# Latent attention in one core's trunk: rotary keys and latent norms placed ahead of the second late modulation piece, the gate's sums placed behind two heads

## The chip, the cores and the metric

The kernel runs on 1 core of one Trainium2 chip. A time is the device time of one execution in microseconds (us). Three executions of the kernel before gave 882.97, 884.5 and 885.7 us; their median, 884.5 us, is what a change is measured against. The core has five engines, each with its own queue of instructions: TensorE (PE in the profile; PEld is its weight load), VectorE (DVE), ScalarE (ACT), GpSimd (POOL) and the sync engine (SP), which here only issues transfers. Engines wait for each other by semaphores.

## What is computed

A trunk of two layers on 256 tokens of width 1024, in float32. Layer 0 is retention and a mixture of experts; layer 1 is latent attention and a mixture of experts. Cut to the part around the change:

```python
mod = c_act @ w_mod[layer] + b_mod[layer]          # six vectors of 1024 for each layer
sh1, sc1, g1, sh2, sc2, g2 = jnp.split(mod, 6, axis=-1)
# layer 1
hn = modulate(rms_norm(h, norm_kv), sh_kv, sc_kv)
a = hn @ w_kv_a                                    # 128 latent + 64 rotary
c_kv = rms_norm(a[..., :128], kv_norm)
k_rope = rope(a[..., 128:])
k_nope, v = split(c_kv @ w_kv_b)                   # 8 heads of 128 + 128
q = rms_norm(modulate(rms_norm(h, norm_mix), sh1, sc1) @ w_q_a, q_norm) @ w_q_b
h = h + g1 * (attention(q, k_nope, k_rope, v) @ w_o)   # g1: the gate of this text
h = h + g2 * grouped_moe(modulate(rms_norm(h, norm_ffn), sh2, sc2), ...)
```

## The kernel before, in words

Every engine's order is written out by hand; nothing is planned at build time. Weights pass through a ring of six slots of 2 MB (`ring`) and some buffers beside it. SP issues the loads in one fixed order, each behind a wait for the use that frees its slot (`released`, L433), so one load that waits holds up all behind it. For layer 1 the order is `MLA_ITEMS` (L126): kva, qa, pieces 20 and 21, kvb, qb, pieces 22 to 25, wo0, wo1, pieces 26 and 27, then the experts' matrices of layer 1 (L483 to L504). Piece 25 takes the slot of piece 21 (freed when `mod_sum` reaches 22), wo0 that of kvb, wo1 that of qb, piece 26 that of piece 22 (`mod_sum` 23), piece 27 that of piece 23 (`mod_sum` 24).

A modulation vector of 1024 is one product of the activated c with a 1024 x 1024 block of `w_mod`. It comes in two pieces (an even and an odd number) of 2 MB. `mod_main` (L1527) has DVE multiply a piece in four quarters, each one instruction on 128x1024 elements that adds to a running sum in `part`; a step waits for the one before. The first quarter of an even piece writes without adding. Pieces 20 and 21 are vector 10, g1 of layer 1; 22 and 23 are vector 11 and 24 and 25 vector 12, shift and scale of the feed-forward of layer 1; 26 and 27 are its gate. What is left is a sum over the 128 partitions, which PE does: `gate_sum` (L610) for a gate (two matmuls of 128x512, one for each half, each two records in the profile), after which DVE's `gate_store` (L1553) adds the bias and stores it into `gate`; `row_sum` (L617) for a shift or scale. After the row sums of vectors 11 and 12 ACT copies the rows and sends them through two small transfers (`copy_rows(3)`, L1222, L1233, `turned<-y`), 4 KB each; DVE's `vectors(3)` (L1674, L1565) and ACT's L1302 wait for them.

The stage around the change, in the order of each engine:

- PE: `hnT` times kva (L1001, key latents and raw rotary keys), `xnT` times qa (L1009, query latents), with the transposes of the raw rotary keys between its halves (L1016); the two sums of vector 10 (L1021 to L1024), which wait for piece 21 and for the rotary products; transposes of the normed latents (L1027, L1032); key up-projection (L1041), its second half behind the gate's stores; value up-projection (L1048); query projections, rotary (L1058) and plain (L1070); then eight heads (L1115: scores L1082 and L1084, transposes of the probabilities L1095, values L1104 to L1106); then the output projection in blocks (L1130), with `row_sum(11)` behind the first block, `row_sum(12)` behind the fourth, and small matmuls of the router (L648, L800); then `experts(1)`, which turns h in four parts (L816), the last one behind `h_ready`.
- DVE: pieces 20 and 21, the rotary key products (L1842), the statistics of the latents (L1846, L1847), the normed latents (L1851, L1853), the query latents with their gain (L1856), the gate's stores (L1559), and then copies of keys and values with quarters of piece 22 between them, rotary query products (L1874), half of piece 23, in the heads the maxima and the scaling (L1881 to L1908), then the second half of piece 23 and pieces 24 to 27, the router's preparation (L1912, L1913), and in `mixed(1)` the four gated blocks of h (L1669), `vectors(3)` ahead of the last.
- ACT: `gate_bias(1)` (L1170, two transfers of the gates' biases into `gate`), modulation, copies of the raw rotary keys (L1360), squares of the latents (L1362, L1365), the root (L1367), the key latents with their gain (L1369), copies, exponentials.
- POOL: copies of the rotary columns of qb (L2071), the rotary keys (L2076 to L2081) behind the key products and the turned latents, the rotary queries (L2084).

Of the kernel before, what the change touches and what calls it, by code (L numbers as in the profile page):

```python
# [85 lines left out]
LATE_MOD = 20  # L86
# [4 lines left out]
MOD_STORED = {}  # L91
# [57 lines left out]
def build_kernel(nc, t, out):  # L149
    with ExitStack() as ctx:  # L150
# [139 lines left out]
        mla_bank = bank[4:] + bank[:4]  # L290
# [257 lines left out]
        def _(pe):  # L548
# [61 lines left out]
            def gate_sum(v, n, b=None):  # L610

                if b is None and (v > FIRST_MOD // 2 or n):
                    pe.wait_ge(mod_stored, MOD_STORED[(v, n)] - 1)
                b = bank[5] if b is None else b
                pe.matmul(b[:], ones, part[:, v % 2, n * 512:(n + 1) * 512], start=True, stop=True).then_inc(mod_folded, 1)
# [404 lines left out]

            pe.wait_ge(mod_sum, LATE_MOD + 2)  # L1021
            pe.wait_ge(kr_mult, 2)
            gate_sum(10, 0, mla_bank[5])
            gate_sum(10, 1, mla_bank[3])  # L1024
            pe.wait_ge(lat_norm, 2)
# [11 lines left out]
            for b in range(4):  # L1037
                if b == 2:
                    pe.wait_ge(mod_stored, MOD_STORED[(10, 1)])
                for j in range(2):  # L1040
                    ins = pe.matmul(mla_bank[1 + b][:, j * SEQ:(j + 1) * SEQ], kvb[:, 2 * b + j, 0:NOPE], ckT, start=True, stop=True)  # L1041
                ins.then_inc(kv_done, 1)
# [72 lines left out]
            for hd in range(MH):  # L1115
                if hd + 2 < MH:
                    scores(hd + 2)
                turn_probs(hd)
                if hd:
                    attend(hd - 1)  # L1120
            attend(MH - 1)

# [28 lines left out]
        def _(act):  # L1151
# [128 lines left out]
            def experts(l):  # L1280
# [71 lines left out]
              scale=rstd[:, 1:2]).then_inc(y1_ready, 1)  # L1352
            act.wait_ge(gb_in, 32)
            gate_bias(1)
            modulate(2, hnT, 4, MOD_COL[2])
# [12 lines left out]
            act.wait_ge(lat_turned, 1)  # L1368
            A(ckT, mla_bank[7][:, 0:SEQ], ACT.Copy, scale=lat_gain[:, 0:1]).then_inc(ckT_ready, 1)  # L1369
            act.wait_ge(rope_w, 1)  # L1370
            for b in (1, 3):
# [47 lines left out]
        def _(dve):  # L1419
# [416 lines left out]
            mod_main(20)  # L1836
            mod_main(21)

            dve.wait_ge(kr_raw, 1)
            for i in range(2):  # L1840
                w = trig[:, 1, i:i + 1, :].to_broadcast([P, 2, SEQ])
                dve.tensor_tensor(mprod[:, i, :].rearrange("p (f s) -> p f s", f=2),  # L1842
                                  mla_bank[5][:].rearrange("p (f s) -> p f s", f=2), w, ALU.mult).then_inc(kr_mult, 1)

            dve.wait_ge(lat_sq, 4)
            dve.tensor_scalar(var[:, 0:2], msq[:, 0:2], 1.0 / KVL, EPS, ALU.mult, ALU.add).then_inc(lat_ms, 1)  # L1846
# [8 lines left out]
            for j in range(2):  # L1855
                dve.tensor_scalar(qaT[:, j, :], mla_bank[0][:, j * SEQ:(j + 1) * SEQ], lat_gain[:, 1 + j:2 + j], None, ALU.mult).then_inc(qaT_ready, 1)  # L1856
            gate_store(10, 0, mla_bank[5])
            gate_store(10, 1, mla_bank[3])
            for b in (2, 4):
                mod_main(22, (b // 2 - 1,))  # L1860
                dve.wait_ge(rope_w, 1)
                dve.wait_ge(kv_done, b)
                dve.tensor_copy(knT[:, 2 * (b - 1):2 * b, :], mla_bank[b][:].rearrange("p (k s) -> p k s", k=2)).then_inc(kv_dve, 1)
            for b in (1, 3):
                dve.wait_ge(kv_done, 4 + b + 1)
                dve.tensor_copy(vm[:, b // 2, 512:1024], mla_bank[(5, 6, 7, 0)[b]][:]).then_inc(kv_dve, 1)
            mod_main(22, (2, 3))

            dve.wait_ge(kr_ready, 5)
            for f in range(2):  # L1870
                dve.wait_ge(qb_done, 1 + f)
                for i in range(2):
                    w = trig[:, 1, i:i + 1, :].to_broadcast([P, 2, SEQ])
                    dve.tensor_tensor(mprod[:, 2 * f + i, :].rearrange("p (f s) -> p f s", f=2),  # L1874
                                      mla_bank[5 + f][:].rearrange("p (f s) -> p f s", f=2), w, ALU.mult).then_inc(qr_mult, 1)
            mod_main(23, (0, 1))
            for b in (2, 4):
# [27 lines left out]
            for hd in range(MH):  # L1905
                head_scale(hd)
                if hd + 2 < MH:
                    head_max(hd + 2)  # L1908
            mod_main(23, (2, 3))
            for m in range(24, N_MOD):  # L1910
# [198 lines left out]
```

## Time and profile before

| | us |
|---|---|
| median of 3 runs | 884.5 |
| lowest, highest | 882.97, 885.7 |
| span of the profiled execution | 882.1 |
| PE busy | 839.5 (95%) |
| DVE busy | 329.5 (37%) |
| ACT busy | 177.4 (20%) |
| POOL busy | 159.5 (18%) |
| mean rate of the DMA engines | 360 GB/s |

The span is that from the first to the last instruction of one profiled execution; no separate time of that execution is given, so the span is what durations are summed against, and it lies 2.4 us under the median and 0.9 under the lowest run. Times in the views are microseconds from the start of the span. The stage of the change runs from about 512 to 592, the heads from 565.6 to 591, the output projection from 591.6 to 624, and the experts of layer 1 from 636.

### The profile page before, as it was taken

The numbers are of one execution on the slowest core, as the hardware profiler recorded it, in microseconds if no ns is written. First come the engines' busy times: TensorE is split into PE (matmuls) and PEld (weight loads), VectorE is DVE, ScalarE is ACT, GpSimd is POOL, SyncE is SP. The second block draws the span as 40 slices with busy tenths as digits, with TensorE's granted clock in tenths as the row PEclk, the third lists the DMA queues.
The fourth block names the chain that finished last, engine by engine and source line by source line (L and its number), as shares of the span: only waits on it lengthen the run. The fifth ranks groups of instructions, "written<-read, shape, count | busy, mean of one in ns | idle before, by whom it ended". The sixth has DMA issues, their size and how long they took to land.

```text
span 882.1 us, 11781 instructions
## 1 busy us (share of the span) xinstructions
PE 839.5 (95%) x4339; PEld 464.0 (53%) x4339; DVE 329.5 (37%) x598; ACT 177.4 (20%) x356; POOL 159.5 (18%) x269
## 2 busy tenths in 40 slices
PE   6999999999999999999999877999899999999996
PEld 4788444444444555455545445774545555545552
DVE  2825766955302322111112058778511112211114
ACT  2100113111102221122121141240322122112112
POOL 0023000000003521122210113300632211012111
PEclk9999999999999999999999998999999999999999
DMA  8989999998567699999999989929899999989994
GB/s 320 387 312 374 374 365 336 366 380 346 210 263 322 265 391 422 421 421 421 422 422 420 346 325 411 374 100 424 324 361 421 421 421 421 379 325 422 421 400 131
DMA packets 70014, 317.29 MB, mean 360 GB/s; under 512 B 10039, under 2 KB 10170, under 8 KB 44366
## 3 DMA queue, kind: packets, MB, share of 16 engines
q1 hardware_dynamic: 61594, 304.42, 86.1%
q0 software_dynamic: 4976, 8.40, 3.2%
q10 hardware_dynamic: 3396, 3.80, 1.3%
q8 instruction: 34, 0.56, 0.3%
q14 instruction: 14, 0.11, 0.0%
HBM read 311.31 MB, written 15.20 MB: 370 GB/s over the span
## 4 chain that ended last, share of the span: by engine, by line
PE 78%; DMA 9%; SPq 6%; DVE 3%; issue 1%; ACT 1%; ACTq 0%; POOL 0%; DVEq 0%; POOLq 0%
PE bank L735 12%; PE bank L914 10%; PE bank L901 10%; PE bank L932 10%; PE bank L776 6%; PE bank L876 6%; SPq L472 6%; PE bank L676 5%; DMA ring<-in_moe_w_down 3%; PE bank L1130 3%; DMA part<-outs 3%; DMA ring<-in_w_mod 2%; PE bank L728 2%; PE bank L557 1%; PE bank L1084 1%
## 5 line engine op out<-in xcount | busy, mean ns | idle before, releaser
L1793 DVE TENSOR_TENSOR arena<-bank,arena 128x256 f32<-128x256 f32 x34 | 20.9, 616 | 253.8 <-PE bank L914 253.8
L1543 DVE SCALAR_TENSOR_TENSOR part<-ring,cpad,part 128x1024 f32<-128x1024 f32 x84 | 111.1, 1323 | 3.3 <-DVE part L1543 0.5
L735 PE MATMUL bank<-ring,xnT 128*128 128x512 f32 x256 | 111.2, 592 | 0.0
L901 PE MATMUL bank<-ring,arena 128*64 128x512 f32 x416 | 92.1, 595 | 0.0
L914 PE MATMUL bank<-ring,arena 128*64 128x256 f32 x704 | 80.3, 381 | 0.2 <-issue 0.2
L932 PE MATMUL bank<-ring,arena 128*64 128x512 f32 x352 | 79.8, 595 | 0.0
L735 PEld LDWEIGHTS bank<-ring,xnT 128*128 128x128 f32 x256 | 48.4, 190 | 59.4 <-issue 59.3
L876 PEld LDWEIGHTS bank<-arena,y 128*128 128x128 f32 x544 | 63.7, 195 | 14.3 <-issue 14.3
L876 PE MATMUL bank<-arena,y 128*128 128x128 f32 x544 | 66.4, 281 | 0.0
L914 PEld LDWEIGHTS bank<-ring,arena 128*64 128x64 f32 x704 | 50.2, 137 | 30.1 <-issue 8.6
L1318 ACT ACTIVATE arena<-bank,modc,scale 128x128 f32<-128x128 f32 x68 | 25.6, 457 | 180.4 <-PE bank L876 176.4
L901 PEld LDWEIGHTS bank<-ring,arena 128*64 128x64 f32 x416 | 28.7, 137 | 52.2 <-issue 52.0
L1970 POOL DMA_INDIRECT outs<-arena,row_id x17 | 18.0, 1060 | 204.4 <-DVE arena L1813 123.7
L1946 POOL TENSOR_TENSOR h<-h,acc 128x512 f32<-128x512 f32 x6 | 7.6, 1267 | 242.0 <-DVE acc L1669 242.0
L1813 DVE SCALAR_TENSOR_TENSOR arena<-bank,info,gate 128x512 f32<-128x512 f32 x34 | 25.4, 751 | 66.3 <-PE bank L932 66.2
L1965 POOL TENSOR_SCALAR arena<-slot_id,place_two 128x64 f32<-128x64 f32 x108 | 45.9, 446 | 5.5 <-POOL slot_id L1980 3.0
L932 PEld LDWEIGHTS bank<-ring,arena 128*64 128x64 f32 x352 | 24.3, 137 | 41.1 <-issue 39.5
L676 PE MATMUL bank<-xnT,ring 128*128 128x256 f32 x192 | 41.9, 379 | 0.0
L676 PEld LDWEIGHTS bank<-xnT,ring 128*128 128x128 f32 x192 | 36.4, 190 | 5.3 <-DVE xnT L1496 0.5
L932 PE MATMUL bank<-arena 128*64 128x512 f32 x120 | 36.3, 596 | 0.0
L914 PE MATMUL bank<-arena 128*64 128x256 f32 x192 | 30.9, 397 | 4.0 <-DMA acc<-in_moe_w_up 4.0
L1784 DVE TENSOR_SCALAR arena<-bank,scale,modc 128x128 f32<-128x128 f32 x68 | 23.2, 406 | 23.6 <-PE bank L876 23.6
(342 smaller groups left out, 1067.6 us busy)
## 6 DMA issues: line engine op xcount, KB each, us to landing
ring<-in_w_mod SPq DMA_DIRECT2D x48, 1024.0 KB, 12.4
ring<-in_moe_w_gate SPq DMA_DIRECT2D x48, 1024.0 KB, 15.4
ring<-in_moe_w_down SPq DMA_DIRECT2D x44, 1024.0 KB, 13.2
ring<-in_moe_w_up SPq DMA_DIRECT2D x40, 1024.0 KB, 12.7
ring<-in_ret_w_in SPq DMA_DIRECT2D x24, 1024.0 KB, 7.5
arena<-in_moe_w_down SPq DMA_DIRECT2D x12, 1024.0 KB, 18.4
arena<-in_moe_w_up SPq DMA_DIRECT2D x12, 1024.0 KB, 17.7
arena<-in_moe_w_gate SPq DMA_DIRECT2D x9, 1024.0 KB, 10.0
```

The source lines that it names most:

```text
L472: sp.dma_start(home(l, m, f), w).then_inc(landed[f][b] if b < RING else outside_in[f][b - RING], 16)
L676: ins = pe.matmul(o[:, f * SEQ:(f + 1) * SEQ], w[:, k, c:c + P], xnT[:, k, :], start=(f == 0 and k == 0), stop=(f == 1 and k == KT - 1))
L735: ins = pe.matmul(pair[tt][:], xnT[:, k, tok(tt)], w[:, k, :], start=(k == 0), stop=(k == KT - 1))
L776: ins = pe.matmul(bank[2 * tt + n][:], yT(4 * i + kk)[:, tok(tt)], w[:, kk, n * 512:(n + 1) * 512], start=(i == 0 and kk == 0), stop=(i == ...
L876: ins = pe.matmul(bank[4 + k // 4][:, (k % 4) * P:(k % 4 + 1) * P], y[:, tt, k * P:(k + 1) * P], chosen_slots[:, tt, :], start=(tt == 0), ...
L901: ins = pe.matmul(bank[0][e * 64:(e + 1) * 64, :], xgT[:, k, e * 64:(e + 1) * 64], w(e, k), start=(k == 0), stop=(k == KT - 1))
L914: ins = pe.matmul(bank[1 + f][e * 64:(e + 1) * 64, 0:256], xgT[:, k, e * 64:(e + 1) * 64], w(2 + e, k)[:, f * 256:(f + 1) * 256], start=(k ...
L932: ins = pe.matmul(bank[6 + n2][e * 64:(e + 1) * 64, :], hidT[:, k, e * 64:(e + 1) * 64], w(4 + e, k)[:, n2 * 512:(n2 + 1) * 512], start=(k ...
L1130: ins = pe.matmul(mla_bank[(5, 7, 0, 4)[2 * tt + n]][:], oT[:, 4 * i + kk, tok(tt)], w[:, kk, n * 512:(n + 1) * 512], start=(i == 0 and kk ...
L1318: ins = A(xgT[:, k, :], bank[5][:, tok(j)], ACT.Identity, bias=modc[:, MOD_COL[l] + 24 + k:MOD_COL[l] + 25 + k], scale=scale[:, 1 + 2 * l, ...
L1543: ins = dve.scalar_tensor_tensor(o, w[:, k, :], c, o, ALU.mult, ALU.add)
L1965: ins = pool.tensor_scalar(dst[:, tt, e * SLOTS:(e + 1) * SLOTS], slots, places[:, tt, e:e + 1], None, ALU.is_equal)
```

## The change

PE no longer does the two sums of vector 10 ahead of the transposes of the latents, and the key up-projection no longer waits for the gate's stores; the sums stand behind heads 0 and 3, into another bank, and DVE stores them behind heads 1 and 4. On DVE the rotary key products and the latent norms come ahead of piece 21, of which one quarter stays in front of the statistics; two quarters take the places that quarters of piece 22 had between the copies, and the fourth the place of the last half of 22. Half of piece 22 takes the place of half of 23. Behind the heads stand half of 22 and all of 23, where half of 23 stood. ACT issues the bias transfers behind the key latents' copy.

```diff
 # PE
-            pe.wait_ge(mod_sum, LATE_MOD + 2)
-            pe.wait_ge(kr_mult, 2)
-            gate_sum(10, 0, mla_bank[5])
-            gate_sum(10, 1, mla_bank[3])
             pe.wait_ge(lat_norm, 2)
...
             for b in range(4):
-                if b == 2:
-                    pe.wait_ge(mod_stored, MOD_STORED[(10, 1)])
                 for j in range(2):
...
                 if hd:
                     attend(hd - 1)
+                if hd == 0:
+                    pe.wait_ge(mod_sum, LATE_MOD + 2)
+                if hd in (0, 3):
+                    gate_sum(10, hd // 3, mla_bank[6])
             attend(MH - 1)
 # ACT
-            act.wait_ge(gb_in, 32)
-            gate_bias(1)
             modulate(2, hnT, 4, MOD_COL[2])
...
             A(ckT, mla_bank[7][:, 0:SEQ], ACT.Copy, scale=lat_gain[:, 0:1]).then_inc(ckT_ready, 1)
+            act.wait_ge(gb_in, 32)
+            gate_bias(1)
             act.wait_ge(rope_w, 1)
 # DVE
             mod_main(20)
-            mod_main(21)
 
             dve.wait_ge(kr_raw, 1)
...
+            mod_main(21, (0,))
             dve.wait_ge(lat_sq, 4)
...
-            gate_store(10, 0, mla_bank[5])
-            gate_store(10, 1, mla_bank[3])
             for b in (2, 4):
-                mod_main(22, (b // 2 - 1,))
+                mod_main(21, (b // 2,))
...
-            mod_main(22, (2, 3))
+            mod_main(21, (3,))
...
-            mod_main(23, (0, 1))
+            mod_main(22, (0, 1))
...
                 if hd + 2 < MH:
                     head_max(hd + 2)
-            mod_main(23, (2, 3))
+                if hd in (1, 4):
+                    gate_store(10, hd // 4, mla_bank[6])
+            mod_main(22, (2, 3))
+            mod_main(23)
             for m in range(24, N_MOD):
                 mod_main(m)
```

## Rows read from the trace of the kernel before

**Rows 1.** The page, busy us of each engine, share of the span and instructions.
```profile
PE 839.5 (95%) x4339; PEld 464.0 (53%) x4339; DVE 329.5 (37%) x598; ACT 177.4 (20%) x356; POOL 159.5 (18%) x269
```
**Rows 2.** The chain that ended last, 517 to 558: start, us, what.
```profile
517.29 16.45 DMA ring<-in_w_mod
...
539.08 1.21 DVE acc L1842 x2
...
540.43 3.75 PE bank L615 x4
...
544.61 0.83 PE bank L1032 x4
...
546.34 1.21 DVE gate L1559 x2
...
547.59 1.99 PE bank L1041 x8
549.58 3.45 PE bank L1048 x8
...
554.00 3.70 PE bank L1058 x16
```
**Rows 3.** Timeline, 529 to 543: start, us, engine, line, operation [idle before <- releaser].
```profile
529.50 3.92 DVE L1543 SCALAR_TENSOR_TENSOR part<-ring,cpad,part 128x1024 f32<-128x1024 f32 x3
...
532.03 0.60 PE L1016 MATMUL bank<-cst,ring 128*128 128x128 f32 x4
...
536.12 0.38 ACT L1365 ACTIVATE xnT<-bank 128x256 f32<-128x256 f32 x1 [6.17 <-PE bank L1009]
...
540.26 0.58 DVE L1847 TENSOR_SCALAR stat<-stat 128x2 f32<-128x2 f32 x1
...
541.34 0.61 DVE L1851 TENSOR_SCALAR arena<-bank,stat 128x128 f32<-128x128 f32 x2
```
**Rows 4.** Windows: us, busy of PE, PEld, DVE, ACT, POOL, granted clock, DMA share, GB/s.
```profile
536.00:538.40 2.40, 0.08 (x1) 0.00 (x0) 2.33 (x3) 0.84 (x4) 0.00 (x0) 1.00 1.03 423
538.40:545.20 6.80, 4.77 (x10) 2.49 (x10) 4.02 (x10) 0.68 (x2) 1.18 (x2) 0.50 1.02 409
...
565.60:586.00 20.40, 20.40 (x137) 18.67 (x138) 11.04 (x54) 9.97 (x37) 0.00 (x0) 1.00 0.54 206
```
**Rows 5.** Timeline, POOL's last rotary key piece and DVE's rotary query products.
```profile
553.98 1.70 POOL L2081 TENSOR_TENSOR xnT<-acc 32x256 f32<-32x256 f32 x1
...
556.99 2.48 DVE L1874 TENSOR_TENSOR acc<-bank,arena 128x512 f32<-128x512 f32 x4 [0.23 <-DVE part L1543]
```
**Rows 6.** Timeline, DVE's wait in one head of four alike.
```profile
583.03 0.35 DVE L1889 TENSOR_SCALAR bank<-bank 64x64 f32<-64x64 f32 x2 [1.23 <-PE bank L1084]
```
**Rows 7.** Timeline of DVE behind the heads: rest of piece 23, piece 25.
```profile
588.88 2.60 DVE L1543 SCALAR_TENSOR_TENSOR part<-ring,cpad,part 128x1024 f32<-128x1024 f32 x2
...
596.34 5.25 DVE L1543 SCALAR_TENSOR_TENSOR part<-ring,cpad,part 128x1024 f32<-128x1024 f32 x4 [0.23 <-DVE part L1543]
```
**Rows 8.** The chain that ended last: the row sums.
```profile
595.28 0.98 PE bank L622 x4
...
606.76 0.98 PE bank L622 x4
```
**Rows 9.** Timeline of SP's queue: loads of pieces 26 and 27.
```profile
565.60 26.80 SPq L423 DMA_DIRECT2D ring<-in_w_mod  x4
```
**Rows 10.** Windows, columns as in Rows 4, around the end of the big queue.
```profile
612.00:620.50 8.50, 8.50 (x31) 4.66 (x31) 2.88 (x8) 1.47 (x4) 2.53 (x2) 1.00 1.01 417
620.50:621.80 1.30, 1.30 (x4) 0.58 (x4) 0.54 (x1) 0.16 (x1) 0.68 (x1) 1.00 0.23 62
```
**Rows 11.** Timeline: the small transfers, DVE's wait for them, the last gated block.
```profile
608.41 1.60 ACTq L1233 DMA_DIRECT2D turned<-y  x2
...
621.81 0.62 DVE L1565 TENSOR_TENSOR modc<-turned,cols 128x16 f32<-128x16 f32 x1 [0.77 <-DMA turned<-y]
...
624.00 0.69 DVE L1669 TENSOR_TENSOR acc<-bank,gate 128x512 f32<-128x512 f32 x1 [0.68 <-PE bank L1130]
```

## The prediction

> **What bounds the kernel now.** I read the busy times first: TensorE (PE) is busy for 95% of the span [rows 1], so the time is PE's queue plus the places where PE stands still. The chain of waits says where it stands still in the part that is edited [rows 2]. The stage begins with a transfer of modulation weights that lands at 533.74; VectorE (DVE) multiplies that piece (four quarters of 1.3 us, not shown one by one), then makes the two rotary-key products at 539.08, and only then may PE do the two sums of the gate at 540.43, the transposes of the latents, half of the key up-projection, wait for the gate's stores at 546.34, and go on. The reader is to see that from 533.74 to 547.59 each step is released by DVE, not by PE's own work.
>
> The timeline of the same stretch says what DVE's order holds up [rows 3]. ACT finished the squares of the latents at 536.96 (the row shown and its like behind it). The statistics that read them ran at 540.26, 3.2 us later, since DVE had first to end piece 21 and the products. Their first result, the normed key latents, was there at 541.95, the query latents about 0.8 later, and PE was by then in the gate's sums, which ran at the low clock: 0.50 of full from 538.4 to 545.2, after PE had had nothing to do from 536.1 on [rows 4]. In the heads that follow PE has no hole: 20.40 of 20.40 us busy [rows 4].
>
> **The front, part by part.** On DVE the products now wait only for their transposes, which PE had done at 532.6 [rows 3], and one quarter of piece 21 goes between them and the statistics: piece 20 ends at 533.4 [rows 3], products 1.3, quarter 1.3, 536.0 at the latest. So the statistics start when ACT is done, at 537.0 in place of 540.2. The same chain behind them (1.7 us to the last normed key latent) puts that at 538.75 against 541.95, and the query latents at 539.5. PE does the transposes until 540.4, against 545.4: it has no gate sums ahead of them (3.75 us [rows 2]) and starts them sooner. The key up-projection is 16 records of 0.25 us at full clock (1.99 for 8 [rows 2]), 0.45 at half clock (the sums took 3.75 for what takes 1.7 at full clock). If the clock stays low until 545.2 as before, 11 records are slow and it ends at 546.5; if it rises one step earlier, near 541.9, it ends at 545.0. Before it ended at 549.58, with a stop of 0.8 for the gate's stores in the middle. Behind it the value projection (3.45) and DVE's last copy (0.7) move along, and the query projection starts at 549.5 to 551.0 in place of 554.0. Gain 3.0 to 4.5; the clock never falling would give 5.7. I take 4.0, since PE is now idle for only 2.7 us but then has thin work.
>
> The removed sums are a warm-up as well, which speaks against the change. The Trainium skill ("TensorE: Matmul & The Clock Gate", Why this matters for your kernels) advises to keep PE free of long gaps, since the clock then falls, and the trace agrees that it fell in such a gap [rows 4]. By that rule alone one would take the gain of 3.0, and the sum below would be 1.0 higher.
>
> DVE keeps up: ahead of each of the copies of keys it has one quarter of piece 21 where it had one of piece 22, and two stores of 0.6 are gone. GpSimd's rotary keys ended at 555.7, 1.3 ahead of their readers [rows 5]; they wait for the turned latents and come forward with them. ACT's two bias transfers cost its queue about 1 us, now behind the key latent's copy and ahead of the first kv copy; that copy's matmuls take PE over 1 us, so they cost nothing; if uncovered, 0.5. Their megabyte leaves the crowded start and joins the queue at 540, ahead of piece 22, which DVE read right behind the stores (547.55 [rows 2]) and now reads 7 us later.
>
> **In the heads** PE gets the two sums. Both stand in its queue where it is never idle, at full clock: 4 records at 0.43 (3.45 for 8 of that shape [rows 2]), **+1.7** (1.5 to 1.9). DVE's two stores of 0.6 fall into its waits, 1.23 per head from the fourth head on [rows 6]; nothing.
>
> **Behind the heads.** Here the displaced work comes due. Let T be where DVE ends head 7 and starts on modulation, 588.88 [rows 7]. Before, half of piece 23 was left: 2.6 us. Now half of 22 and all of 23 are left: 2.6 + 5.25 = 7.85. PE asks for both at T + 6.4, its first row sum at 595.28 [rows 8], and now waits 1.5 us. Pieces 24 and 25 are ready at T + 18.3, PE asks for them at T + 17.9 + 1.5: no second wait.
>
> The sync engine's queue is moved too. Its load into piece 22's slot waits for that piece: it went out at 565.60 [rows 9], during the heads, when the DMA engines had room (share 0.54 [rows 4]); it now goes at T + 2.6, and the next one, which before went out with the end of piece 23 at T + 2.6, the end of the same row [rows 9], now goes at T + 7.9. All expert loads of the second layer queue behind it. That queue kept the engines full (417 GB/s) until 620.5 [rows 10]; now everything in it is 5.3 us later, ending at T + 36.9. The first expert runs from 636 on, so by themselves they cost nothing. But one tiny transfer hangs on that queue: the turned modulation rows of the last feed-forward, issued by ACT at 608.41, were read at 621.81 after a wait [rows 11]: twice 4 KB took 13 us and ended right when the big queue ran dry. I take it that they do so again, 5.4 later against T. DVE stands in that wait ahead of the fourth gated block of h; it had 0.9 to spare there (the chain from 621.81 to 624.00 is 1.2 us of work [rows 11]). So h is complete 4.4 us later against T, routing starts 4.4 later, and the 1.5 of the row sum is inside it. **+4.4**; bounds +1.5 (transfer not held) and +6 (held a microsecond more).
>
> **Sum**: 4.0 gained, 1.7 and 4.4 lost: +2.1 on a span of 882.1, 884.2. The runs' median is 884.5, 2.4 above that span, so 886.6. Between the ends: 5.7 gained, 1.5 + 1.5 lost is -2.7 (881.8); 3.0 gained, 1.9 + 6 lost is +4.9 (889.4). 0.3% (about 2.65 us) is what a measurement can tell from no change; my number is inside it, near its upper edge (887.2).
>
> **Rivals.**
> 1. *The tiny transfer meets the next flood* (slower). PE's last output block frees the slot of the next load: T + 35.1, where DVE stopped waiting for it [rows 11], and the 1.5 that PE is late, T + 36.6, with data half a microsecond on, while the old queue ends at T + 36.9. If the idle moment in which the small one finished (share 0.23 from 620.5 to 621.8 [rows 10]) no longer exists, it is held until those 7.3 MB are in, 17 us more: about +19, 903. For it: the margin is under 1 us. Against: new loads start thinly. It decides once the old queue ends more than about 1 us later than I count.
> 2. *The tiny transfer isn't held by the queue.* Then only PE's 1.5 stays: -4.0 + 1.7 + 1.5 = -0.8, 883.7. For: in the trace the two ends could coincide by chance. Against: the wait ended within a microsecond of the queue. The Trainium skill ("DMA: Bandwidth & Descriptors", Queues, rings and completion order) says that each DMA engine takes turns between queues with work, a packet at a time; by that rule a few kilobytes wouldn't wait for megabytes to end, and this rival's time would be the right one.
> 3. *The front gains its all* (faster): the clock stays up, 5.7, and the transfer comes in time: -5.7 + 1.7 + 1.5 = -2.5, 882.0, and a little under it if DVE's backlog is shorter than counted. For: PE's hole shrinks from 4.3 us to 2.7. Against: it needs both, and the clock fell 2.4 us into the last one.
>
> **Chances.** The forecast's mechanism 0.62 (of it 0.34 within 0.3%, 0.28 slower; its own range 883.8 to 889.4); rival 1 0.12, slower; rival 2 0.15 (0.11 within, 0.04 faster); rival 3 0.11 (0.08 faster, 0.03 within). So faster 0.12, same 0.48, slower 0.40. The range, 882.5 to 890.5, leaves out rival 1 and most of the faster cases.
>
> **What would show it.** Right: DVE's key products at about 533 to 534, the statistics at 537, PE's transposes at 538.8, no sum between 536 and 549; the query projection 3 to 4.5 earlier; two sums of 0.86 in the heads; an idle spell of 1.5 on PE at its first row sum, released by DVE; two weight loads issued behind the heads; DVE waiting 4 us or more for the turned rows, and PE idle by about 3 in its turns of h. Wrong: the turned rows landing while the big queue is still full (rival 2), landing near 640 (rival 1), or the query projection under 3 or over 5 earlier.

## Result and profile after

The changed kernel takes 888.01 us (median of 8 executions, 884.63 to 889.92); the kernel before, measured beside it, 883.28 (8 executions, 881.99 to 885.7). The ratio is 1.0045, 95% interval 1.0027 to 1.0063: slower by 4 us. The forecast was 886.6 with a range of 882.5 to 890.5.

The profiled execution was the fastest of the eight: 884.63 us, span 882.9, against a span of 882.1 before. In every execution that has both, the time lies 1.7 to 1.8 us above the span, so the profile before belongs to an execution of about 883.8 us (an estimate), near its median. So the two profiles differ by 0.8 us where the medians differ by 4.7; a good part of what follows is about that gap.

The front of the stage, in the chain of waits of the changed kernel (start, us, what):

```profile
536.67 0.17 DVE stat L1844
...
537.39 0.61 DVE arena L1849 x2
...
538.84 1.11 PE bank L1028 x4
539.95 4.21 PE bank L1035 x16
544.16 3.45 PE bank L1042 x8
...
548.59 3.71 PE bank L1052 x16
```

Against [rows 2] and [rows 3]: the statistics start at 536.67 in place of 540.26, the key up-projection (L1035, before L1041) runs in one piece, and the query projection (L1052, before L1058) starts at 548.59 in place of 554.00, 5.41 us sooner, of which 0.39 was gained before the stage began.

The timeline of VectorE and of the sync engine's queue behind the heads, in the changed kernel (start, us, engine, line, operation):

```profile
585.18 2.60 DVE L1541 SCALAR_TENSOR_TENSOR part<-ring,cpad,part 128x1024 f32<-128x1024 f32 x2
587.87 6.30 SPq L423 DMA_DIRECT2D ring<-in_w_mod  x4
588.01 5.25 DVE L1541 SCALAR_TENSOR_TENSOR part<-ring,cpad,part 128x1024 f32<-128x1024 f32 x4 [0.23 <-DVE part L1541]
593.31 1.05 PE L622 MATMUL bank<-part,cst 128*32 128x512 f32 x4 [1.73 <-DVE part L1541]
594.21 2.22 SPq L472 DMA_DIRECT2D arena<-in_moe_w_down  x3
```

T, where VectorE has ended the heads and begins on modulation, is 585.18 here and was 588.88 [rows 7]. Half of piece 22 and all of piece 23 follow, TensorE stands still for 1.73 us at its first row sum, and the two loads of piece 26, issued at 565.60 before [rows 9], go out at 587.87; those of piece 27 follow at 593.28.

The end of the stage, same view, and the window behind it (us, busy time of PE, PEld, DVE, ACT, POOL, granted clock, DMA share, GB/s):

```profile
606.51 1.59 ACTq L1231 DMA_DIRECT2D turned<-y  x2
...
623.47 0.18 DVE L1563 TENSOR_TENSOR modc<-turned,cols 128x16 f32<-128x16 f32 x1 [4.33 <-DMA turned<-y]
...
625.96 0.63 PE L816 MATMUL bank<-cst,h 128*128 128x128 f32 x4 [2.59 <-DVE h L1681]
```

```profile
612.00:622.60 10.60, 10.60 (x32) 5.05 (x32) 4.64 (x10) 2.29 (x7) 3.75 (x3) 1.00 0.99 409
622.60:623.40 0.80, 0.78 (x8) 0.54 (x5) 0.00 (x0) 0.80 (x2) 0.00 (x0) 1.00 0.83 159
626.70:633.50 6.80, 6.27 (x41) 3.23 (x33) 3.65 (x17) 2.04 (x4) 6.11 (x4) 0.50 1.01 424
```

VectorE waits 4.33 us for the turned modulation rows where it waited 0.77 [rows 11]. The small transfer was issued 1.9 us sooner than before and read 1.66 us later, 0.9 us after the full stretch of the DMA engines ended. The last four turns of h wait 2.59 us behind it, and TensorE's clock is at half from 626.7 on, for 6.8 us.

**A ledger.** To compare executions I count from the moment at which VectorE adds the first layer's result to h, since what lies ahead of it is the same code. "Again" is a second profile of each kernel, runs e0 and e1 below. The numbers are us from one mark to the next; each mark is the start of a row in the timeline (for the turns of h, of the last L816 row).

| stretch | before | changed | before, again | changed, again |
|---|---|---|---|---|
| TensorE's key-latent projection (L1001), itself | 5.44 | 5.44 | 6.83 | 7.07 |
| h added, to the query projection | 42.36 | 37.34 | 39.04 | 39.57 |
| to the output projection (query projections and heads) | 37.61 | 39.31 | 37.59 | 39.32 |
| to the last turns of h | 33.97 | 38.06 | 33.98 | 38.52 |
| to the first expert (routing) | 15.05 | 15.34 | 14.45 | 15.55 |
| together | 128.99 | 130.05 | 125.06 | 132.96 |

From the first expert (its first matmul with the ring's weights, L901) to the end all four take 241.4 to 241.6 us. In the first pair the change costs 1.1 us, in the second 7.9. Neither pair is typical: the first has the fastest of the changed kernel's timed executions, the second, with 880.19 us, one faster than every other timed execution of the kernel before (880.37 to 886.24). The two typical ones, the first column against the last, differ by 4.0 in this ledger, near the medians' 4.7: -2.8 in the front, +1.7, +4.6 and +0.5.

### The profile page after: what moved, and what is told of

It is laid out like the page before. It is cut to its first block, busy times and chain, and to the rows that moved or that the text cites. A ratio compares the mean times of both kernels' runs of the same rounds, so it can differ in the third digit from the quotient of the medians.

```text
span 882.9 us, 11781 instructions
## 1 busy us (share of the span) xinstructions
PE 839.5 (95%) x4339; PEld 464.3 (53%) x4339; DVE 327.4 (37%) x598; ACT 177.1 (20%) x356; POOL 156.8 (18%) x269
## 4 chain that ended last, share of the span: by engine, by line
PE 74%; DMA 12%; SPq 5%; DVE 4%; issue 2%; ACT 1%; ACTq 0%; POOL 0%; DVEq 0%; POOLq 0%
PE bank L735 12%; PE bank L914 10%; PE bank L901 10%; PE bank L932 10%; PE bank L776 6%; SPq L472 5%; PE bank L676 5%; PE bank L876 5%; DMA ring<-in_moe_w_down 3%; DMA ring<-in_moe_w_up 3%; DMA part<-outs 3%; DMA turned<-y 2%; PE bank L728 2%; PE bank L1128 1%; PE bank L1078 1%
## 5 line engine op out<-in xcount | busy, mean ns | idle before, releaser
L901 PE MATMUL bank<-ring,arena 128*64 128x512 f32 x416 | 92.1, 595 | 0.7 <-DVE arena L1782 0.7
L901 PEld LDWEIGHTS bank<-ring,arena 128*64 128x64 f32 x416 | 28.7, 137 | 52.9 <-issue 52.0
```

What stands on the lines that cost most here:

```text
L901: ins = pe.matmul(bank[0][e * 64:(e + 1) * 64, :], xgT[:, k, e * 64:(e + 1) * 64], w(e, k), start=(k == 0), stop=(k == KT - 1))
```

## Experiments

### e1 and e0: each kernel once more

e1 is the changed kernel with nothing edited, e0 the kernel before, executed once.

> The changed kernel once more, nothing edited. In its profiled execution the stage behind the heads cost 4.3 us more than before and the front gained 5.0, yet the medians lie 4.7 us apart and that execution was the fastest of its eight. Theory A (the clock): the mechanism is the same in all executions and the rest is which stretches TensorE does at 1.2 GHz. Then this look has the turned rows landing within 1.5 us of the end of the big queue again, and any time above 884.6 shows as matmuls at the low clock between 536 and 560 or between 620 and 645. Theory B (the flood): in the slower executions the turned rows are caught by the next loads; then DVE waits 6 to 20 us for them in place of 4.3. Median expected 887 to 889 by either.

> The kernel before once more, for a second look at which stretches TensorE does at the low clock. Four of the five later looks at changed kernels had it low at about 520 to 527, in the key latents' projection, where neither the first look at before nor the one at the changed kernel had it; that costs 1.6 to 2 us. If it is a matter of where in time the kernel falls, before shows it too in some executions and its front then starts 1.6 later; if the moved bias transfers cause it, before doesn't show it.

e1: 888.85 us (6 executions), ratio 1.0051 (1.0034 to 1.0068), profiled 889.43. Theory B fell: in this slow execution the turned rows were waited for 4.80 us, much as in the fast one, and no timed execution is over 890.12, where a flood would add some 17. e0: 880.19. Their timelines of TensorE, first e0:

```profile
524.10 6.83 PE L1001 MATMUL bank<-ring,arena 128*128 128x192 f32 x32 [1.26 <-DVE xnT L1454]
...
539.43 1.96 PE L615 MATMUL bank<-part,cst 128*128 128x512 f32 x4 [1.16 <-DVE acc L1842]
...
542.28 1.95 PE L1041 MATMUL bank<-arena,ring 128*128 128x256 f32 x8
```

and e1:

```profile
525.49 7.07 PE L1001 MATMUL bank<-ring,arena 128*128 128x192 f32 x32 [1.26 <-DVE xnT L1452]
...
542.27 0.56 PE L1023 MATMUL bank<-cst,arena 128*128 128x128 f32 x2 [2.37 <-DVE arena L1849]
...
543.97 4.56 PE L1035 MATMUL bank<-arena,ring 128*128 128x256 f32 x16
```

In both, TensorE had half its clock around 520 to 529 (windows: e0 0.50 from 520.1 to 526.9, e1 0.50 from 522.0 to 528.8). Both kernels can fall there and both can stay at full clock, as the first two profiles show; so the edit alone doesn't bring it. But it goes with what the edit is worth. With TensorE that much later, more of VectorE's work on piece 21 lies beside TensorE's own projections (TensorE waits 1.16 us ahead of the sums in place of 4.34), that work begins 1.4 us sooner counted from the mark, and the gate's sums find TensorE at full clock: they take 1.96 us where they took 3.75 [rows 2]. The front of the kernel before gets 3.3 us shorter, half clock in the projection and all. The changed kernel waits for the same late projection, then for ScalarE and VectorE, stands still for 2.37 us, and falls to half clock at 542.5 for 3.4 us. The front's gain of 5.0 us becomes a loss of 0.5.

Some of the runs below leave this front as it is, so there are more profiles of it. With the code before it took 42.36, 39.04 and 39.06 us (before, e0, e10), with the changed code 37.34, 39.57, 40.34 and 39.46 (changed, e1, e2, e4). The means differ by 1.0 us, not by the 4.0 of the forecast; with so few executions that is no more than a pointer, but with +1.7 and +4.4 it comes to the 4.7 of the medians within half a microsecond.

### e2: nobody on the path reads the turned rows

```diff
 DVE, at the last gated block of h
-                if l:
-                    vectors(3, cols[:, :, 10:12])
-                    scales(3, MOD_COL[1] + 32, gcol[:, :, 3])
 DVE, ahead of the experts
+                if l:
+                    vectors(3, cols[:, :, 10:12])
+                    scales(3, MOD_COL[1] + 32, gcol[:, :, 3])
 ACT, the square that would overwrite the transfer's source
-                    act.wait_ge(vecs_in, 128)
-                    act.wait_ge(vecs_turned, 2)
-                A(y[:, 1, 512:1024], h
+                A(y[:, 1, 0:512], h
```

(GpSimd's last routing block and ScalarE's first expert now carry the waits.)

> The changed kernel, but nobody on the path to routing reads the turned rows of the last feed-forward: DVE adds them to their biases behind routing, the square on ScalarE writes elsewhere, and GpSimd's second half of y waits for them. If the small transfer is what cost 2.7 of the 4.3 us behind the heads, this is 2.7 faster than the changed kernel (885.3 against 888.0) in the median, TensorE's last turn of h waits under 0.5 us, and what is left against before is the 1.7 us at the first row sum. If the medians differ for another reason (clock), it is less than 1 us faster. If the flood caught the rows in some executions, it is 4 or more faster.

883.72 us (12 executions), ratio 1.0002 (0.9988 to 1.0016): 4 to 5 us under the changed kernel, more than the 2.7 expected and the whole loss. Its profile is its slowest execution (887.03) and of the kind with half clock in the projection, so it stands against e1: from the output projection to the last turns of h 35.78 us against 38.52, routing 14.87 against 15.55, and no slow stretch in routing at all. The wait was worth 2.7, and routing took 0.7 less without its slow stretch; the remaining 1.8 over the kernel before is the row sum. The rest of the gain in the times isn't located. It goes with the clock: the mean granted clock is 0.988 to 0.992 in the eleven other executions of e2, 0.981 to 0.986 in all of the changed kernel's but the fastest.

### e10: the same edit in the kernel before

> The kernel before with the readers of the turned vector rows moved as in e2 (VectorE reads them ahead of the last experts, ScalarE's square writes elsewhere, GpSimd waits at its last block). A control for e2: in the kernel before, VectorE waits 0.77 us for those rows (and the rest of what stands between the attention and the router is the same), so if e2 gained because the rows were late there, this gains 0.5 to 1 us against the kernel before, and no more. If e2's move is good in itself (a shorter VectorE queue at the stage's end, whatever the transfer does), this gains as much as e2 did against the changed kernel, 3 to 5 us.

884.07 us (11), ratio 0.9998 (0.9987 to 1.0009). No gain that can be measured (up to 1.1 us isn't excluded), against the 0.5 to 1 expected, and far from e2's 4 to 5: on the kernel before, where the rows come in time, the edit is worth little or nothing. In its profile routing has a slow stretch of 6.8 us (from 631.5) and takes 16.72 us, though nothing waits for the rows.

### e4: the turned rows freed by another queue order

```diff
-                if l:
-                    outside_down()
                 for j in range(4):
                     ...
-                if l == 0:
-                    outside_down()
+                outside_down()
```

> The changed kernel, with 3 MB of the next layer's down matrices issued behind the four gate and up loads of the first pair in place of ahead of them, so that the queue ahead of the turned rows is 3 MB shorter. If the small transfer is held until the big queue is dry, it lands about 6 us sooner (near 617 in place of 623.3), DVE doesn't wait for it, and the kernel is 2.7 us faster than the changed one (885.3), like the one with the rows read late. If the transfer takes its 15 to 17 us from its issue whatever is queued, it is within 0.5 of the changed one (888.0). Risk: the down matrices of the first pair come too late for it, which would show as a wait of TensorE at its first down projection.

891.69 us (5), ratio 1.0082 (1.0061 to 1.0102): slower still, where 885.3 had been expected. The first half came true. With three megabyte loads fewer ahead of it the queue ran dry sooner, the turned rows were read at 622.25 without a wait, and the last turns of h waited 0.30. But the moved loads were then in the way later: from 640 to 660 the DMA engines were full (share 1.02; 0.76 in e1 for the same work), and GpSimd's scatter of results took long, in the chain of waits of e4:

```profile
641.36 0.98 DMA outs<-arena,back_id
...
648.35 11.67 DMA outs<-arena,row_id
```

TensorE waited 1.02 us behind the scatter (at 664.26), and later for a matrix of the experts, in the timeline of e4:

```profile
757.05 5.19 PE L912 MATMUL bank<-ring,arena 128*64 128x256 f32 x34 [3.79 <-DMA ring<-in_moe_w_up]
```

From the first expert to the end it took 247.7 us, 6 more than any other version; these two waits are 4.8 of them. The wait at the first down projection, which had been named as the risk, didn't come; the backlog showed elsewhere.

### e3: the gate's bias transfers alone

The kernel before, with only ScalarE's two bias transfers moved behind the key latent's copy.

```diff
-            act.wait_ge(gb_in, 32)
-            gate_bias(1)
             modulate(2, hnT, 4, MOD_COL[2])
             ...
             A(ckT, mla_bank[7][:, 0:SEQ], ACT.Copy, scale=lat_gain[:, 0:1]).then_inc(ckT_ready, 1)
+            act.wait_ge(gb_in, 32)
+            gate_bias(1)
```

> The kernel before with one edit: the two bias transfers go out behind the key latents' copy. Theory: the first link of the chain before was the landing of piece 21 at 533.74, behind that megabyte; without it pieces 20 and 21 land 2.5 us sooner, DVE's chain starts 2.3 sooner and PE's gate sums stand at 538.1 in place of 540.4: 2.0 to 2.4 us faster than before. Rival (what the prediction said: this edit costs and gains nothing, the gain comes from the order on DVE): within 0.5 us of before.

891.49 us (6), ratio 1.0089 (1.0074 to 1.0103). My expectation was wrong by 10 us. Its first half held in part: VectorE starts on piece 21 1.3 us sooner, counted from the mark, than in e0 and e10. The timeline of e3 says where the rest went:

```profile
540.40 0.85 ACTq L1172 DMA_DIRECT2D gate<-in_b_mod  x2
...
551.20 1.29 DVE L1559 TENSOR_TENSOR gate<-bank,gate 128x512 f32<-128x512 f32 x2 [8.93 <-DMA gate<-in_b_mod]
552.54 3.06 PEld L1041 LDWEIGHTS bank<-arena,ring 128*128 128x128 f32 x8 [9.86 <-DVE gate L1559]
```

The megabyte beside a full weight queue took 10.3 us here, and the gate's store needs it; TensorE waits behind the store. The store in the changed kernel comes at 570.57, in a head, long after. So nothing waits for the late transfers there, because the stores have left the front with them: the edits hold each other up.

### e8: VectorE's order put back

The changed kernel (sums in the heads, bias late), with pieces 21, 22 and 23 multiplied where the kernel before has them.

```diff
             mod_main(20)
+            mod_main(21)
 ...
-            mod_main(21, (0,))
 ...
-                mod_main(21, (b // 2,))
+                mod_main(22, (b // 2 - 1,))
 ...
-            mod_main(21, (3,))
+            mod_main(22, (2, 3))
 ...
-            mod_main(22, (0, 1))
+            mod_main(23, (0, 1))
```

> The changed kernel with DVE's order of products put back: all of piece 21 ahead of the rotary key products and the statistics, piece 22 between the copies, half of 23 ahead of the heads and half behind. The sums stay in the heads, the bias transfers stay late. Theory: DVE's order is worth only about 1 us in the front (statistics at 537.7 in place of 536.7, since piece 21 lands 2.5 sooner anyhow), and all of the 4.3 us behind the heads is its price. So this is 3 us or more faster than the changed kernel (884.5 or less) and 1.5 to 3 faster than before: no wait at the first row sum, turned rows read as in before. Rival (what the change's name says): the order on DVE is what frees the front; then the query projection stands within 1.5 us of where before had it and the time is 883 to 885.

883.3 us (11), ratio 0.9996 (0.9986 to 1.0006). It is over 3 us faster than the changed kernel, as expected, but not faster than the kernel before. The moves of the gate's sums and of the bias transfers are together worth nothing measurable, and VectorE's reordering on top of them costs the 5 us. e8's profile is again of the kind with half clock in the projection: 39.76 us to the query projection, a wait of 0.65 for the turned rows. And there VectorE's order held up nothing in the front, in the timeline of e8:

```profile
540.08 0.17 DVE L1844 TENSOR_SCALAR stat<-stat 128x2 f32<-128x2 f32 x1 [2.47 <-ACT xnT L1361]
```

With all of piece 21 and the key products ahead of them, the statistics still wait 2.47 us for ScalarE's squares. So in an execution of this kind the edit that gives the change its name frees nothing: the changed front took 39.57, 40.34 and 39.46.

### e5 and e6: the new order without its price

e5 keeps the keys and norms ahead of piece 21, and puts every displaced quarter into a wait that VectorE already has in the front and in heads 2 and 3, so that behind the heads as little is left as before.

```diff
-            mod_main(21, (0,))
+            mod_main(21, (0, 1))
 ...
-                mod_main(21, (b // 2,))
+                mod_main(21, (b // 2 + 1,))
 ...
-            mod_main(21, (3,))
+            mod_main(22, (0,))
 ...
-            mod_main(22, (0, 1))
+            mod_main(22, (1,))
 (behind each copy of queries)
+                mod_main(22, (b // 2 + 1,))
 (in the heads)
+                if hd in (2, 3):
+                    mod_main(23, (hd - 2,))
-            mod_main(22, (2, 3))
-            mod_main(23)
+            mod_main(23, (2, 3))
```

> The changed kernel with the quarters of pieces 21 to 23 put where its DVE stood still (two ahead of the statistics, one between and one behind the query copies, two in heads 2 and 3), so that piece 22 is done before the heads and half of 23 before their end, as in before. If the 4.3 us behind the heads come from displaced work alone, the row sum waits for nothing, the big queue ends as in before and the turned rows with it: 4 us faster than the changed kernel, 884 or less, and 3 faster than before in the profiles (front -5, heads +1.7). The quarters in the heads cost PE 0.3 at most. If it is slower than that, DVE's waits in the heads were not free.

883.52 us (11), ratio 0.9994 (0.9983 to 1.0005), 4.5 to 5.3 us under the changed kernel by the medians, as expected. Its profile has the front's gain (37.40) and none of the loss behind the heads (no wait at the row sum, 0.75 us for the turned rows), but the heads still carry the sums, and with the quarters in them they take 39.81 against 39.31: 0.5, where 0.3 at most was expected.

e6 is e5 with the two sums in TensorE's stops: one ahead of the rotary query projection, where it waits 0.99 us for VectorE's copies, one ahead of head 0. VectorE stores the first among its rotary query products and the second in head 1. The part on TensorE:

```diff
+            pe.wait_ge(mod_sum, LATE_MOD + 2)
+            pe.wait_ge(kv_dve, 1)
+            gate_sum(10, 0, mla_bank[2])
             pe.wait_ge(kv_act, 4)
 ...
             pe.wait_ge(qr_mult, 4)
+            gate_sum(10, 1, mla_bank[6])
 ...
-                if hd in (0, 3):
-                    gate_sum(10, hd // 3, mla_bank[6])
```

> As the one with the quarters in DVE's waits, and the two sums of the gate out of the heads: the first into PE's stop ahead of the rotary query projection (0.95 us), the second into its stop ahead of head 0 (0.94). Each sum is 0.86 long. If PE's queue bounds the heads without a gap, this is 1.5 us faster than the one before. Risk: the bias transfers land at 548 to 550 and the first store waits for them, which would show as TensorE waiting for the gate's store in the plain query projection.

882.02 us (12), ratio 0.9984 (0.9973 to 0.9995), 1.5 us under e5, as expected. In its profile, its fastest execution (878.8), the stretch of the heads takes 37.98 us, against 39.81 in e5 and 37.61 before, the front 37.21, and TensorE waits for no gate store.

### e11: TensorE kept busy where it stood still

```diff
             ins.then_inc(kr_raw, 1)
+            keep_warm(4, 7)
 
             pe.wait_ge(lat_norm, 2)
```

> The changed kernel with four spare matmuls of 512 columns (1.9 us at 2.4 GHz by the value projection's row, 3.5 at 1.2) on TensorE between the query-latent projection and the latent transposes, where the second profile of the changed kernel shows it idle for 2.37 us (up to 542.27) and then at the slow clock for 3.4 us. Theory (the idle stretch costs the clock, since the gate's sums that stood there in the kernel before are gone): the slow stretch at 542 is gone, the key up-projection takes 4.0 us in place of 4.56 and the transposes less by 0.1 or so; the change's loss goes down by 0.5 to 1.5 us, so 0.5 to 1.5 us under the changed kernel. Rival (the clock falls there whatever TensorE does in the gap): key up-projection 4.2 to 4.6 as now and no difference in the time, or up to 1 us longer where the spare matmuls run slowly and the transposes queue behind them.

886.12 us (12), ratio 1.0032 (1.0016 to 1.0049). The changed kernel's two ratios are 1.0045 and 1.0051, so by the ratios it gains 1.1 to 1.7 us, by the medians 1.9 to 2.7; the intervals overlap. Its timeline:

```profile
537.57 3.60 PE L557 MATMUL bank<-cst 128*128 128x512 f32 x8
541.00 0.38 PE L1024 MATMUL bank<-cst,arena 128*128 128x128 f32 x2
...
542.04 3.69 PE L1036 MATMUL bank<-arena,ring 128*128 128x256 f32 x16 [0.22 <-ACT arena L1366]
```

No slow stretch there, and the key up-projection at 3.69 against 4.56. But the spare matmuls fill 3.6 us, twice what I had counted (each is two records), and the norms were there about 1 us before the transposes began at 541.00; two would have been enough. This profile has the projection at full clock, and its query projection comes after 37.49 us, no better than the changed kernel's first profile (37.34). So the slow stretch is gone, as foretold, and the times have the foretold sign, but the gain isn't clear of noise; that it sits in executions of e1's kind is likely, not shown. The slow stretch behind the turned rows (628.6, 6.8 us) and the wait for them (4.77) are untouched.

### e7 and e12: everything together

e7 is e6 with e2's edit.

> e6 (gate sums in TensorE's stops of the front, VectorE's pieces as in e5) with the readers of the turned vector rows moved as in e2. In e6 the time to the start of the last experts is 1.4 us under that of the kernel before in the same kind of execution. If e2's gain was the late rows alone and e6 has them in time (its profile shows the wait at L1563's line under 1 us), the two together give e6's time within 1 us: 882. If the gain of e2 is in the shorter queue, the two add: 878 to 880.

880.74 us (12), ratio 0.9964 (0.9951 to 0.9977): faster than the kernel before by 3.2 us, and the best version measured. e6, against its own runs of before, stood at 0.9984; the further gain is 1.3 to 1.8 us, between my two expectations. That is more than e10 showed for the same edit, though e6 too has the rows in time (a wait of 0.73); why, these runs don't say.

e12 is e7 with e11's spare matmuls.

> e7 with the four spare matmuls of e11. In e7's profile TensorE is idle for 2.37 us before the latent transposes and has the slow clock from 539.3 for 3.4 us; its transposes take 0.69 and 1.12 us and its key up-projection 4.40, against 0.38, 0.60 and 3.69 in e11. Theory (the idle stretch costs the clock): 1.2 to 1.5 us faster than e7, 879.4 us, and no slow stretch at 539. Rival (the fall of the clock merely moves to the next gap, the 1 us at the rotary query projection or the first heads, or the spare matmuls delay the transposes): 0 to 1 us slower than e7, 881 to 882 us, with a slow stretch between 545 and 560.

880.91 us (6), ratio 0.9966 (0.9952 to 0.9979): no different from e7, where 879.4 had been expected. The query projection came 0.43 us sooner after the stage's start (36.71 against 37.14), but the clock fell later instead, in routing. The same line in e12's timeline and then in e7's:

```profile
629.52 3.76 PE L557 MATMUL bank<-cst 128*128 128x512 f32 x4
```

```profile
629.32 1.96 PE L557 MATMUL bank<-cst 128*128 128x512 f32 x4
```

Both kernels have the same code and the same gaps there. One execution of each doesn't show that one fall causes the other; it does show, as e10 did, that a slow stretch can appear in routing without a late transfer.

## Why the prediction was right, and where it was not

**The statistics and the norms.** Foretold at 537.0 and 538.75 to 539.5; seen at 536.67 and 538.79. Right. The key products started at 532.27, before the 533 to 534 foretold, as soon as their transposes were there: piece 20 was begun at 526.41, which had been 528.71.

**The front, -4.0 (bounds 3.0 to 4.5, 5.7 with the clock up).** This term was mis-sized. In the profiled pair it was -5.0, and the query projection stood 5.41 us earlier, over the 5 that the prediction had named as a sign of being wrong: the clock fell at 537.9 and was back after 3.4 us, 0.6 us sooner than in its better case. In the second pair it was +0.5, and over all profiles of the two fronts -1.0. The term was read from one execution, in which the sums ran at half clock and took 3.75 us, and was used for the median. The removed sums were a warm-up as well, the doubt that I had named and priced at 1.0: e0 with them has no slow stretch at the norms, e1 without them has one, and e11, with busy work back in their place, has none. The advice of the Trainium skill ("TensorE: Matmul & The Clock Gate", Why this matters for your kernels) against long gaps agrees in kind with e1's fall at 542.5, but the standstill, 2.37 us, was shorter than the gaps that it warns of; how often an execution falls there, no run here settles. One working of the prediction doesn't hold either: 3.75 against 1.7 us makes a record of 0.25 us one of 0.55 at half clock, not 0.45. The 0.45 itself was near: in e3 eight of them took 3.78 us, 0.47 each.

**The heads, +1.7.** Right: +1.70 and +1.73, the length of the two sums; VectorE's stores (0.69 each) added nothing to it.

**Behind the heads, +4.4.** Right. From T to the first expert it was 51.75 and is 56.12: +4.4. Row sum 1.73 (foretold 1.5), loads at T + 2.7 and T + 8.1 (foretold 2.6 and 7.9), the big queue dry near T + 37.4 (36.9). e5, which takes the displaced work away, and e8, which puts VectorE's order back, both lose this cost, and e2 shows what part of it is the turned rows. Not foretold was the clock in routing. The three profiles with a wait of 2.6 to 3.1 us at the turns of h (changed, e1, e11) all fall to half clock right behind it, for 6.8 us each. But of the eleven others five have a slow stretch in routing too (before, e5 and e8 3.4 us, e10 and e12 6.8), so the +0.3 and +1.1 of the two pairs aren't the wait's alone.

**The bias transfers, nothing.** No run changes them alone in the changed kernel. Its profile agrees with nothing lost, since the first store comes at 570.57, long after they land, but the reason that I gave (ScalarE's queue has room) was beside the point: where something waits for their landing it costs a wait of 8.93 us, and 7.7 us of the kernel's time, as e3 shows.

**The rivals.** Rival 1, the next flood catching the small transfer, didn't occur: it landed 0.9 us after the queue ran dry. Rival 3 had a front gain of 5.7 and the transfer in time; the front came near it in one execution, the transfer didn't. Rival 2, the small transfer not held, fell. The rule of the Trainium skill that I set behind it ("DMA: Bandwidth & Descriptors", Queues, rings and completion order) is that an engine takes turns between queues, a packet at a time. Here is the view of the DMA queues of the changed kernel, 612 to 617 and then 622.6 to 623.5 (queue, packets, MB, share of 16 engines):

```profile
q1 hardware_dynamic: 289, 2.11, 101.6%
q10 hardware_dynamic: 35, 0.00, 0.5%
```

```profile
q1 hardware_dynamic: 20, 0.12, 64.4%
q10 hardware_dynamic: 144, 0.00, 9.0%
```

From 607.5 to 623.5 the small queue moves 260 packets in all, since its 8 KB are sent in rows of 8 elements. Beside the full queue it gets 7 packets in each us, one for some 8 of the other's, each of those over 200 times as large; at that rate 260 would take 37 us. As the big queue runs dry, 144 go in 0.9 us. The kernel before has the same picture: 57 packets in the 12 us from 608.5 on, 203 in the 1.3 us from 620.5 on. So the small queue is served beside the full one, and it is late because it is small in bytes and large in pieces; that the engines take turns is my reading of these counts, and no run sent the same 8 KB in fewer pieces. The page has a turn drain typically 9 to 17 descriptors of one ring. For the big queue eight comes near that. For the small one it doesn't hold here: by it the small queue's pieces, some 16 for each of the 16 engines if they are spread evenly, would be through in a turn or two, and the counts show one piece for each eight of the other's. The measurement decides. My step from the rule to "a few kilobytes don't wait" was the mistake, and the measured 13 us [rows 11] had rightly been given more weight.

**The sum.** -4.0 + 1.7 + 4.4 = +2.1. Profiled pair: -5.0 + 1.7 + 4.1 + 0.3 = +1.1. Second pair: +0.5 + 1.7 + 4.5 + 1.1 = +7.9 (from unrounded terms). The median moved by 4.7, between them. So the direction and both costs were right, and the number landed near with some luck: the change was 2.6 us larger than foretold, the kernel before was 1.2 us faster in this measurement than the 884.5 that the forecast was counted from, and 888.01 came out 1.4 above 886.6. The heavier weight on "no change that can be measured" (0.48, against 0.40 for slower) rested in part on the front of the one profile of the kernel before, the longest of its three. Why an execution falls to half clock at 520 us and another not stays open: it was not steered in any run, and e0, e1, e2, e3, e4, e8 and e10 have that stretch, the two first profiles, e5, e6, e7 and e12 don't, and e11 has half of it.

## What to carry to other kernels

Take a stage's gain from more than one execution when the clock had fallen in it: a stop at half clock is one that another execution may not have, and the same edit was worth -5.0 and +0.5 us. Work that leaves a critical stretch must be followed to where it comes due, with every load and small transfer that waits for it; here spreading the displaced quarters over waits (e5) or taking the readers of a late transfer off the path (e2) each took away the whole loss of 4.7 us, and both together, with the sums in TensorE's stops (e7), made it a gain of 3.2. Count a small transfer that shares the DMA engines with a full queue by its pieces, not by its bytes.

## What the runs showed of the hardware that I had not expected

- 8 KB in 260 packets moved at 7 packets per us beside the full queue and at about 160 per us as it ran dry (144 in 0.9; 203 in 1.3 in the kernel before). By contrast the bias rows, 4 KB pieces, moved 223 packets and 0.85 MB from 542 to 549 in e3, a third of the engines' time (34.6%), beside 453 of the weight queue.
- TensorE work in a stretch where it waits for others can keep the clock up: with four spare matmuls in the place of the gate's sums (e11) the stretch of 3.4 us at half clock was gone there. What that is worth isn't settled: 1 to 3 us less in the changed kernel, with overlapping intervals, and nothing in e12, where the fall came 89 us later, in routing.
- Two executions of one kernel differed by 3.9 us from the stage's start to the first expert (128.99 and 125.06 before) and by 2.9 (130.05 and 132.96) after the change, in opposite directions between the same two kinds of execution.
